# A hybrid attention layer in one kernel: data for three stage borders fetched ahead, two stores put behind loads, and a change of order on GpSimd

## The reference

```
h    = LN(x)                                        # 2064 x 1024
proj = h @ w_in                                     # 1024 x 4040 columns: q,k,v | q,latent,indexer | gates
A    = windowed attention with sinks over the last chunks of 64 and the meta tokens (8 heads)
B    = top-256 selection by an indexer score, then attention over the chosen latents (8 heads)
mix  = (sigmoid(gA) * (A @ w_o_a) + sigmoid(gB) * (B @ w_o_b)) @ w_out
h    = LN(2**0.25 * h + mix)
out  = LN(2**0.25 * h + (silu(h @ w_gate) * (h @ w_up)) @ w_down)     # d_ff 2816
```

## Time and profile before

| | us |
|---|---|
| three runs | 3702.49, 3703.35, 3707.95 (median 3703.35) |
| the profiled execution, its own time | 3713.29 |
| its span, first to last instruction | 3711.0 |
| PE busy | 3479.2 (94%) |
| DVE, ACT, POOL busy | 2222.7 (60%), 1925.1 (52%), 1701.6 (46%) |
| mean granted PE clock, share of full | 0.978 |
| DMA queues q1 (SP) and q10 (ACT), share of 16 engines | 32.1%, 5.7% |

### The profile page before, as it was taken

How to read it: one execution, slowest core, us unless ns; L and a number is a source line. 1 busy time by engine, 2 the same in 40 slices (tenths; PEclk the granted TensorE clock), 3 DMA queues, 4 the chain that set the end, 5 groups by cost and what they waited for, 6 DMA issues and landing times. The chain is left out here.

```text
span 3711.0 us, 52572 instructions
## 1 busy us (share of the span) xinstructions
PE 3479.2 (94%) x17924; PEld 2900.8 (78%) x17924; DVE 2222.7 (60%) x3097; ACT 1925.1 (52%) x3592; POOL 1701.6 (46%) x1806
## 2 busy tenths in 40 slices
PE   6988998898989999999997998999999999999997
PEld 5776777777767888988996777778887888888786
DVE  5236888787632565676533666764546545565867
ACT  3223787788635798887553332343334333344443
POOL 5342344765311322222004665556664665554756
PEclk9999999999989999999998999999999999999998
DMA  8344324332221111100005445654445444365663
GB/s 272 130 132 113 98 83 133 113 92 79 79 74 44 40 42 35 35 20 16 23 11 187 165 169 177 227 199 149 168 141 195 153 142 151 129 246 190 236 227 132
DMA packets 338458, 468.44 MB, mean 126 GB/s; under 512 B 23184, under 2 KB 225120, under 8 KB 334992
## 3 DMA queue, kind: packets, MB, share of 16 engines
q1 hardware_dynamic: 310064, 387.47, 32.1%
q10 hardware_dynamic: 28128, 77.60, 5.7%
HBM read 311.21 MB, written 153.78 MB: 125 GB/s over the span
## 5 line engine op out<-in xcount | busy, mean ns | idle before, releaser
L2629 POOL TENSOR_TENSOR ff_rounded_ring<-ff_raw,ff_rounded_ring 128x512 fp32r<-128x512 f32 x264 | 383.1, 1462 | 294.8 <-ACT ff_rounded_ring L2776 292.1
L100 PE MATMUL ff_bank<-ff_rounded_pair,ff_rounded_ring 128*128 128x512 f32 x1232 | 484.3, 393 | 17.7 <-POOL ff_rounded_ring L2629 12.8
L101 PE MATMUL ff_bank<-ff_rounded_pair,ff_rounded_ring 128*128 128x512 f32 x1232 | 482.9, 392 | 0.0
L102 PE MATMUL ff_bank<-ff_rounded_pair,ff_rounded_ring 128*128 128x512 f32 x1232 | 482.5, 392 | 0.0
L1796 PE MATMUL at_ctx<-at_p_t,at_c_nat 128*128 128x128 f32 (+1 forms) x2432 | 344.1, 282 | 8.1 <-ACT at_ctx_t L1912 7.3
L1796 PEld LDWEIGHTS at_ctx<-at_p_t,at_c_nat 128*128 128x128 f32 (+1 forms) x2432 | 300.7, 191 | 35.4 <-ACT at_ctx_t L1912 13.0
L1906 ACT ACTIVATE at_p_t<-at_turn 128x512 f32<-128x512 f32 (+4 forms) x416 | 213.1, 544 | 206.8 <-PE at_turn L1773 176.8
L2634 POOL TENSOR_TENSOR ff_rounded_ring<-ff_raw,ff_rounded_ring 128x512 fp32r<-128x512 f32 x154 | 212.2, 1383 | 174.6 <-ACT ff_rounded_ring L2826 174.6
L3057 DVE TENSOR_TENSOR ff_rounded_a_ring<-ff_f_q,ff_rounded_a_ring 128x512 fp32r<-128x512 f32 x154 | 210.1, 1374 | 130.8 <-ACT ff_rounded_a_ring L2818 129.7
L100 PEld LDWEIGHTS ff_bank<-ff_rounded_pair,ff_rounded_ring 128*128 128x128 f32 x1232 | 233.5, 190 | 69.8 <-POOL ff_rounded_ring L2629 14.8
L102 PEld LDWEIGHTS ff_bank<-ff_rounded_pair,ff_rounded_ring 128*128 128x128 f32 x1232 | 233.5, 190 | 48.8
(11 more groups left out here) (389 smaller groups left out, 9078.6 us busy)
## 6 DMA issues: line engine op xcount, KB each, us to landing
f_kept<-ff_resid SPq DMA_DIRECT2D x154, 256.0 KB, 2.4
ff_f_q<-f_kept ACTq DMA_DIRECT2D x12, 2816.0 KB, 11.0
pj_raw<-in_w_in SPq DMA_DIRECT2D x58, 512.0 KB, 4.5
proj<-se_row SPq DMA_DIRECT2D x104, 256.0 KB, 2.6
ff_raw<-in_w_ff_gate SPq DMA_DIRECT2D x22, 1024.0 KB, 10.8
ff_raw<-in_w_ff_up SPq DMA_DIRECT2D x22, 1024.0 KB, 6.2
ff_raw<-down_comb SPq DMA_DIRECT2D x88, 256.0 KB, 2.7
ff_raw<-in_w_ff_down SPq DMA_DIRECT2D x66, 256.0 KB, 3.0
```

The lines of the kernel that those rows point to most:

```text
L100: pe.matmul(out, lhs_lo, rhs_hi, start=start, stop=False, skip_group_check=goes_on)
L101: pe.matmul(out, lhs_hi, rhs_hi, start=False, stop=False, skip_group_check=goes_on)
L102: return pe.matmul(out, lhs_hi, rhs_lo, start=False, stop=stop, skip_group_check=goes_on)
L2629: pool.tensor_tensor(ring[:, step % RING, 1, :].rearrange("p (k c) -> p k c", c=P), f_operand(it, q, m), f32(ring[:, step % RING, 0, :]).r ...
```

## The change

- `unit_order`: the first four units of the second half are (0, g0), (1, g0), (0, g1), (1, g1). `SOON` gets the third of them. `load_group` issues eight DMAs of 512 KB in place of two of 2 MB, high and low in turn, and each pair of pieces has a semaphore of its own.
- `attention`: SP's first DMAs stand in another order, `c_nat` is loaded in a first part (3 row blocks of 128) and the rest with semaphores of its own, and PE's first logits wait for the keys alone. `wuv` comes 16th. PE waits for `w_loaded` one step later.
- The mixing stage's first operands are loaded during attention, into a place of their own (`early`): the first 512 columns of `w_o_a` and `w_o_b` at tile 5, and the A half of group 0's attention output at tile 6. `p_t` lies in that place's free part. The rings of the FFN lie there later. Three fp32 matmuls on `early` open PE's list of the stage. `w_o` is held in two halves of columns; a block's high part is one activation of 1024.
- `store_job` is issued at c = 5 and 7, each behind that step's load.
- POOL: `low_weight(step + LEAD)` in front of `inverse_root`.
- `load_raw` of the first two FFN weights waits for the last `low_att` and no longer for `lo_ready`.

```diff
 def unit_order():
-    return units + [(c, g, left + many + k) for k, c in enumerate(OTHERS) for g in (0, 1)], LEFT + 2 * OTHERS, half
+    units += [(OTHERS[k], g, left + many + k) for g in (0, 1) for k in (0, 1)]
+    return units + [(c, g, left + many + 2 + k) for k, c in enumerate(OTHERS[2:]) for g in (0, 1)], LEFT + 2 * OTHERS, half
...
-SOON = (FIRST_HALF - 2, FIRST_HALF - 1)
+SOON = (FIRST_HALF - 2, FIRST_HALF - 1, FIRST_HALF + 2)
...
                     def load_group(g):
                         sp.wait_ge(acc_ready, LAST_OF_GROUP[g + 2] + 1)
-                        sp.dma_start(f32(flat(h_hi[g])), h_kept[g, 0]).then_inc(h_loaded[g], 16)
-                        sp.dma_start(f32(flat(h_lo[g])), h_kept[g, 1]).then_inc(h_loaded[g], 16)
+                        for e in range(KT // 2):
+                            for v, part_of in ((0, h_hi), (1, h_lo)):
+                                sp.dma_start(f32(part_of[g][:, 2 * e:2 * e + 2, :]), h_kept[g, v]...[:, 2 * e:2 * e + 2, :]).then_inc(h_loaded[g][e], 16)
...
-                            if g < 2:
-                                pe.wait_ge(h_loaded[g], 32)
+                        if g < 2 and c % 2 == 0:
+                            pe.wait_ge(h_loaded[g][c // 2], 32)
...
-        p_t = [s.sb(f"p_t{u}", [P, 4, P]) for u in range(PT)]
+        p_t = [early[1][:, KT // 2 + u, :].rearrange("p (m c) -> p m c", m=4) for u in range(PT)]
...
+                first, first_rows = width(1), -(-width(1) // P)
+                load_keys(0, first, 0)
                 load_distances(0)
+                load_natural(0, first_rows, 0)
                 load_distances(1)
+                sp.dma_start(sink_u[:, :], sinks.to_broadcast([P, HEADS])).then_inc(w_loaded, 16)
+                for half in range(2):
+                    sp.dma_start(k_win[half * DH:half * DH + DH, :, 0:META], ...).then_inc(w_loaded, 16)
+                sp.dma_start(v_win[0:META, 0, :], v_nat[PAD:PAD + META, :]).then_inc(w_loaded, 16)
                 load_window(0)
                 load_values(0)
+                sp.dma_start(wuv[:, :, :], w_uv[0].rearrange("h r d -> r h d")).then_inc(w_loaded, 16)
+                load_keys(first, L, 1)
+                load_natural(first_rows, TILES, 1)
+                sp.dma_start(c_nat[0:META, SEQ:SEQ + P], c_nat_kept[SEQ:L, :]).then_inc(nat_loaded[1], 16)
...
+                    if t == 5:
+                        for e, src in enumerate((w_o_a, w_o_b)):
+                            sp.dma_start(early[0][:, 4 * e:4 * e + 4, :], src...[:, :, 0:GROUP]).then_inc(early_loaded[0], 16)
+                    if t == 6:
+                        sp.wait_ge(attn_stored, 32 * TPG)
+                        sp.dma_start(early[1][:, 0:4, :], attn[0:512, 0:GROUP]...).then_inc(early_loaded[1], 16)
...
-                        pe.wait_ge(c_loaded[t // 2], (64, 32)[t // 2])
+                        pe.wait_ge(c_loaded[t // 2], 32)
...
-                load_w_o(0); load_gates(0, 0); load_gates(0, 1); load_w_o(1); ln x 2; load_w_o(2); load_w_o(3)
+                load_gates(0, 0); load_gates(0, 1); load_w_o(0); load_w_o(1); ln x 2
...
-                        if g >= 2 and c in (4, 5):
-                            store_job(2 * g - 8 + c)
+                        if g >= 2 and c in (5, 7):
+                            store_job(2 * g - 4 + c // 7)
...
                 for step in range(F_STEPS):
                     it, r = divmod(step, PER_IT)
+                    if step + LEAD < F_STEPS:
+                        low_weight(step + LEAD)
                     if it == 0 and r in (2, 4, 6, 8):
                         inverse_root(NG - 1, r // 2 - 1)
-                    if step + LEAD < F_STEPS:
-                        low_weight(step + LEAD)
...
-                        for d, src in block_parts(b):
-                            last = act.activation(as_k(w_hi[u])[:, d, :], src, ACT.Copy)
-                        last.then_inc(hi_ready[u], 1)
+                        act.activation(as_k(w_hi[u]), block_part(b), ACT.Copy).then_inc(hi_ready[u], 1)
...
-                    for e in range(2):
+                    for e in range(0 if g else 1, 2):
                         act.dma_start(att[:, 4 * e:4 * e + 4, :], attn[...]).then_inc(att_loaded[e], 16)
...
+                pe.wait_ge(early_loaded[0], 32)
+                for c in range(3):
+                    pe.matmul(bank[:, 2 * pair_at["mix", 0, 0][0], :], early[0][:, c, 0:P], early[0][:, c, :], start=True, stop=True)
```

More of the change, by code:

```diff
@@ L1350, in project_and_select, with attention @@
     return s.all_sems
-def attention(nc, proj, v_nat, wuk_t, w_uv, sinks, attn, c_kept, dist_kept, score, done_with):
+def attention(nc, proj, v_nat, wuk_t, w_uv, sinks, attn, c_kept, dist_kept, score, done_with, early, early_loaded, w_o_a, w_o_b):
     c_nat_kept, c_hi_kept, c_lo_kept = c_kept
@@ L2199, in mix_and_ffn @@
 def mix_and_ffn(nc, proj, attn, h0, h1_turned_d, h1_nat, comb, f_kept, down_comb, w_o_a, w_o_b, w_out, ln1_g, ln1_b, w_gate, w_up, w_down,
-                ln2_g, ln2_b, out, outer):
+                ln2_g, ln2_b, out, outer, first, early, early_loaded, small):
     with Scope(nc, "ff") as s:
@@ L2241, in mix_and_ffn @@
         last_turned_to = [spare[:, :], fstage[:, 3, :]]
-        raw = [raw_all[:, 4 * D + u * D:4 * D + u * D + D] for u in range(2)]
-        w_o_half = [w_o_first[:, :, :], raw_all[:, 0:4 * D].rearrange("p (k c) -> p k c", c=D)]
+        raw = [raw_last[:, u * D:u * D + D] for u in range(2)]
+        w_o_part, att = [early[0][:, :, :], w_o_second[:, :, :]], early[1]
         part_a, part_b, mixed = snap[:, 0, :], snap[:, 1, :], [snap[:, 2 + u, :] for u in range(2)]
@@ L2441, in load_raw @@
                     elif j < 2:
-                        for u in range(2):
-                            sp.wait_ge(lo_ready[u], use1(NG - 1, KT - 2 + u) + 1)
+                        sp.wait_ge(att_lo_ready, KT * NG)
                     else:
@@ L2596, in low_part @@
                     if b < KT:
-                        for d, src in block_parts(b):
-                            last = pool.tensor_tensor(as_k(w_lo[u])[:, d, :], src, as_k(f32(w_hi[u]))[:, d, :], ALU.subtract)
+                        for d in (slice(0, KT // 2), slice(KT // 2, KT)):
+                            last = pool.tensor_tensor(as_k(w_lo[u])[:, d, :], block_part(b)[:, d, :], as_k(f32(w_hi[u]))[:, d, :], ALU.subtract)
                         last.then_inc(lo_ready[u], 1)
@@ L3335, in build @@
     dist_kept = nc.dram_tensor("dist_kept", (TILES, P, L), F32, kind="Internal").ap()
-    with Scope(nc, "out") as outer:
+    with Scope(nc, "out") as outer, Scope(nc, "early") as kept, Scope(nc, "early") as first:
         outer.sems("stored", TPG + 1)
+        early_loaded = kept.sems("loaded")
         with Scope(nc, "late") as s:
@@ L3342, in build @@
                                           late_score, w_uk, wuk_t)
+            small = kept.far("small", [P, 344])
+            early = [first.far(f"half{u}", [P, KT, GROUP]) for u in range(2)]
             if phases > 2:
-                attention(nc, proj, v_nat, wuk_t, w_uv, sinks, attn, c_kept, dist_kept, late_score, done_with)
+                attention(nc, proj, v_nat, wuk_t, w_uv, sinks, attn, c_kept, dist_kept, late_score, done_with, early, early_loaded, w_o_a[0], w_o_b[0])
         if phases > 3:
```

89 lines of the change are left out of this document (45 added, 44 removed).

## The result

| | kernel before | changed kernel |
|---|---|---|
| median of six runs each, us | 3704.60 (3699.65 to 3708.72) | 3679.64 (3673.77 to 3682.96) |
| changed / before | | 0.9928, 95% interval 0.9915 to 0.9940 |
| the same, in a second comparison | 3709.48 | 3685.01; 0.9935, 0.9921 to 0.9949 |

The medians differ by 25.0 us. The ratio 0.9928 of 3704.6 is 26.7 us less, between 22.2 and 31.5. The forecast was 25.6 less, and 3678 for the time.

The account below looks back on a forecast made before the run. PE, busy 3479.2 of 3711.0 us, was taken as the bound, with only idle gaps and half-speed stretches to shorten. Terms −3.4 − 4.5 − 8.1 − 8.9 − 0.7 = −25.6 took the median 3703.35 to 3677.8; range 3665 to 3692.

Parts of the forecast that it names:

- Step 1: Border inside the projection: new unit order saves 6.8 us, a new wait costs 3.4; net −3.4 us, from −8 to 0.
- What is late next: Projection, after the four reordered units: load 2's low part comes late for (2, g0), making PE wait 3.4 us.
- Rival (a): Late transfers in mixing, a wait eating the border's gain, slow clock staying in `project_out(2)`: only −14.8 us, 3688.6; chance 0.14.
- Step 2: Start of attention: DVE's first `latent` no longer waits for the distances; −4.5 us, from −6 to −1.
- Step 3: Start of mixing: operands loaded during attention bring the first block's result earlier; −8.1 us, from −10 to −4.
- Step 4: `project_out(2)`: loads ahead of two stores remove PE's 6.25 us gap and slow clock behind; −8.9 us, from −9.5 to −5.
- Step 5: First FFN iteration, POOL's `low_weight` before `inverse_root`: gaps move rather than go; −0.7 us, from −13 to +5.
- rival (b): First FFN iteration: all PE gaps and slow clock there go, total −37.8 us, 3665.6; chance 0.06.
- rival (d): First attention tiles, 56 us: half-speed clock holds on after the earlier start, up to +14.4 us, 3718; chance 0.04.

Follow-up runs that it names:

- u1: Changed kernel with the old order of units, old `SOON` and two DMAs of 2 MB for a group of `h`: 3683.99 us, 0.9933 of the kernel before.
- u7: Changed kernel without the third entry of `SOON`, new order of units kept: 3683.83 us, 0.9931 of the kernel before.
- u8: Changed kernel with POOL making the second mixing block's low part only after DVE's eight low parts of `att`: 0.9922 of the kernel before.

## Why the prediction was right

By steps, forecast and then measured by the medians of the stretches:

- **Step 1, −3.4: wrong, −0.4.** The four units went as worked out: −7.1 for them (forecast −6.8), then a wait at (2, g0), 2.1 for the 3.4 taken. What failed is the line "What is late next": it looked one load ahead. Two loads further on, ACT's high part and POOL's quarters stand among the search's instructions, and their time is set by the search. PE's lead is given back there (2.10 at 707.45 and the slow matmuls behind it). u1 and u7 show that it is given back, to about 1 us, whatever happens at the border. Rival (a) had this loss in it for another reason.
- **Step 2, −4.5: right, −5.3.** The first latent came when DVE was free, as forecast; `wuv` was no bound. From the end of the projection to the first latent the medians are 22.8 and 18.3, the 4.5 of the forecast. Behind it, from first to fifth latent, all nine profiles with the new order have 10.89, those with the old one 10.83 to 12.50 with a median of 11.3: 0.4 more, not forecast.
- **Step 3, −8.1: right, −9.7.** PE started 4.8 us behind ACT's first DMA of the stage (forecast 4.6) and `att`'s second half landed 6.9 behind it (forecast 8.1 from 1983.4). What the forecast had wrong is what bounds the block. It took the landing and, behind it, ACT and four of DVE's pieces at 1.10. But 1.10 was the mean of pieces of 1.35 to 1.78 beside POOL and of 0.68 without it, and DVE's fourth piece ended only at 1979.34, 1.6 us behind the landing. So the chain of DVE's eight pieces set the result, at the same 8.8 us as before; from the landing to its last piece it was 4.0 us for the 5.0 taken. u8 confirms it: with POOL held back DVE is faster and waits 0.67 for the landing.
- **Step 4, −8.9: right, −10.0,** in both directions and alone.
- **Step 5, −0.7: right in kind, about −2.** The gaps moved from POOL to ACT as forecast, 6.00 in place of 3.71, but the other two nearly vanished in the first profile (1.01; 2.15 in the second). L2995, in the place of L2980, took 1.28 at three of its four places there, 6.1 us in all for 9.2; the pairs of L3026 between them took 3.45, 4.49 and 3.43, 11.4 us in all for 8.2. So the overlap did move to another DVE instruction, as the rule of the Trainium skill quoted in step 5 has it, and DVE gained nothing. By that rule the step would be worth nothing; the likely 2 us are PE's, which waits less for POOL, and nothing at all isn't excluded. A slip in the forecast: 9.0 and 4.6 are 13.6, not 13, so rival (b) stood at 3664.9, just outside the range.
- **The clock of rival (d)** did not fall in its 56 us. It is between 0.85 and 1.00 in that stretch from one execution to the next, with either start. The nine profiles with the new start have a median of 61.8 us and two at 68.7, the five with the old one 63.3 to 68.9. But in tile 2, behind that stretch, PE's clock was 0.82 to 0.86 in four of the nine and 1.00 in all five with the old start; the four lost 4 to 5 us there. From the end of the projection to the last turn of attention the medians are 938.9 and 933.6, 5.2 less, and the means 940.4 and 936.8, only 3.6 less. Whether the new start makes the slow tile 2 more likely stays open with so few profiles.

So the total was right to 1 or 2 us partly by luck: 3.0 of step 1 did not come, and 4.8 more came in steps 2 to 5. Had only step 1's part failed and the others come as forecast, the forecast would have missed by 3, still inside its range.

## What to carry to other kernels

When PE's wait at a border goes, follow the next two or three loads of the same ring, and ask whose list their split stands in: a lead is kept only until the next engine with a pace of its own. A load that stands in a queue behind a store that waits is worth a look first, since moving it costs nothing and here gave the most. Where executions differ by more than a part is worth, take the part out alone and time its stretch between two instructions that both kernels have.

## What the runs showed of the hardware

PE's granted clock over the same instructions was 0.85 to 1.00 in the first tiles of attention, with kernel and time otherwise alike; the stretch from the fifth latent to tile 1 took 61.8 (five profiles) to 68.9. This alone makes 7 us, 0.2% of the kernel, and tile 2 with a clock of 0.82 to 1.00 makes another 5. And a subtraction of 512 columns on DVE with both inputs in SBUF took 0.68 us alone and 1.35 to 1.78 beside one of POOL's; in the mixing stage that set the first product, and not the landing of `att`, for which ACT waits in the profile.
